# Expert layers of the latent tokens: streaming both whole tables and multiplying densely, with the first seven U parts multiplied while the gates are made

## The reference

```python
q = (xt @ lp["peer_wq"]).reshape(n_tok, PEER_HEADS, 2, PEER_HALF)
s = jnp.einsum("thmd,mhnd->thmn", q, lp["peer_keys"])
# per head: top 16 of 128 in each half, top 16 of their 256 sums
idx = ...   # key1 * 128 + key2, 8 heads x 16 picks per token
g = jax.nn.softmax(top_s, axis=-1)
act = jnp.einsum("td,thkd->thk", xb, u_tab[ib])
out = jnp.einsum("thk,thkd->td", jax.nn.gelu(act) * gb, v_tab[ib])
```

## Time and profile before

| | |
|---|---|
| median of three runs | 2433.51 us |
| the profiled execution's own time (its span, from the first to the last instruction) | 2689.8 us |
| TensorE matmul busy | 1510.1 us, 56% |
| VectorE busy | 1524.4 us, 57% |
| ScalarE busy | 281.3 us, 10% |
| POOL busy | 1466.1 us, 55% |
| moved by DMA | 969.43 MB, mean 360 GB/s |
| of it the gathers (queue 0) | 805.40 MB |
| mean granted TensorE clock | 0.721 |

### The profile page before, as it was taken

How to read it: one execution, slowest core, us unless ns; L and a number is a source line. 1 busy time by engine, 2 the same in 40 slices (tenths; PEclk the granted TensorE clock), 3 DMA queues, 4 the chain that set the end, 5 groups by cost and what they waited for, 6 DMA issues and landing times.

```text
span 2689.8 us, 20637 instructions
## 1 busy us (share of the span) xinstructions
PE 1510.1 (56%) x6676; PEld 682.0 (25%) x6676; DVE 1524.4 (57%) x4059; ACT 281.3 (10%) x715; POOL 1466.1 (55%) x1540
## 2 busy tenths in 40 slices
PE   6898668694244554554556866868400444442466
PEld 2464433371012110122312442354100100110012
DVE  0349974756886555455360965575776844446401
ACT  1321133010000110100000032211000000000000
POOL 0005445536665666666556635545676666667664
PEclk8889888896666665676768787878755655565568
DMA  9979998988999999999979988888899999999997
GB/s 360 411 320 379 395 388 324 365 306 318 357 397 411 412 388 379 371 410 411 389 286 374 364 341 314 324 313 296 318 399 373 343 383 375 358 374 383 378 357 271
DMA packets 238044, 969.43 MB, mean 360 GB/s; under 512 B 26314, under 2 KB 28746, under 8 KB 227954
## 3 DMA queue, kind: packets, MB, share of 16 engines
q0 software_dynamic: 221184, 805.40, 78.0%
q1 hardware_dynamic: 16754, 162.71, 14.9%
HBM read 964.87 MB, written 3.15 MB: 360 GB/s over the span
## 4 chain that ended last, share of the span: by engine, by line
DVE 27%; PE 24%; issue 15%; POOL 13%; another core or an unknown queue 11%; DMA 7%; ACT 2%; SPq 0%; DVEq 0%; ACTq 0%; POOLq 0%
PE acc L1077 8%; PE psum L1031 6%; DVE ring L1871 6%; POOL work L695 6%; POOL ring L695 5%; DVE work L1871 3%; PE psum L786 3%; DVE work L1463 2%; POOL wring L695 2%; DMA ring<-peer_v_in,vidx 2%; PE psum L796 2%; DVE work L1460 2%; DMA ring<-peer_u_in,idx 1%; DVE wring L1871 1%
## 5 line engine op out<-in xcount | busy, mean ns | idle before, releaser
L695 POOL DMA_INDIRECT ring<-peer_u_in,idx x415 | 396.5, 955 | 460.6 <-DVE idx L1566 208.0
L1871 DVE CUSTOM_DVE_ANT_0 ring<-ring,h_kept 128x1024 f32<-128x1024 f32 x415 | 488.9, 1218 | 126.3 <-DMA ring<-peer_u_in,idx 93.5
L695 POOL DMA_INDIRECT ring<-peer_v_in,vidx x392 | 378.5, 966 | 325.8 <-PE acc L1077 116.9
L1077 PE MATMUL acc<-ring,vw 128*32 128x512 f32 x1412 | 299.2, 778 | 276.6 <-DVE vw L1852 107.6
L1077 PE MATMUL acc<-work,vw 128*32 128x512 f32 x852 | 218.4, 794 | 325.5 <-DVE vw L1852 155.0
L1871 DVE CUSTOM_DVE_ANT_0 work<-work,h_kept 128x1024 f32<-128x1024 f32 x220 | 262.0, 1219 | 159.3 <-DMA work<-peer_u_in,idx 124.2
L695 POOL DMA_INDIRECT work<-peer_v_in,vidx x267 | 252.0, 944 | 144.8 <-issue 74.0
L695 POOL DMA_INDIRECT work<-peer_u_in,idx x220 | 207.1, 941 | 116.7 <-issue 58.9
L1031 PE MATMUL psum<-work,wring 128*128 128x256 f32 (+1 forms) x896 | 187.1, 369 | 49.5 <-issue 46.6
L786 PE MATMUL psum<-wring,work 128*128 128x512 f32 (+1 forms) x432 | 180.4, 575 | 32.4 <-issue 22.8
L1031 PEld LDWEIGHTS psum<-work,wring 128*128 128x128 f32 x896 | 160.3, 216 | 81.5 <-issue 62.0
(11 more groups left out here) (244 smaller groups left out, 2028.4 us busy)
## 6 DMA issues: line engine op xcount, KB each, us to landing
wring<-w_in_in SPq DMA_DIRECT2D x17, 2048.0 KB
wring<-peer_wq_in SPq DMA_DIRECT2D x14, 2048.0 KB
wring<-mod_w_in SPq DMA_DIRECT2D x10, 2048.0 KB
ring<-mod_w_in SPq DMA_DIRECT2D x9, 2048.0 KB, 12.2
wring<-w_out_in SPq DMA_DIRECT2D x8, 2048.0 KB
work<-mod_w_in SPq DMA_DIRECT2D x5, 2048.0 KB, 14.4
ring<-peer_u_in,idx POOLq DMA_INDIRECT x415
ring<-peer_v_in,vidx POOLq DMA_INDIRECT x392
```

Of the source, the lines that this page charges most:

```text
L695: nc.gpsimd.indirect_dma_start(slots[slot_of[n]], None, table, bass.IndirectOffsetOnAxis(ap=at[:, col + r:col + r + 1], axis=0))\
L1077: ins = mm(acc[half][lane:lane + QUAD, :], w[:, at:at + QUAD], two[j - pair][0][:, half * CHUNK:(half + 1) * CHUNK], start=(r == 0), stop= ...
L1871: V.tensor_tensor_reduce(held, held, h_kept[:, :], 1.0, 0.0, ALU.mult, ALU.add, dots[:, dots_at(k, t) + r:dots_at(k, t) + r + 1]).then_inc ...
```

## The change

Context steps keep the gathers. A latent step no longer gathers:

1. **Gates** (`dense_gates`, new pauses `("gates", t, i)`). For each tile the picks' key1, key2 and gates are transposed to one pick per partition. For each token, VectorE makes a 128 x 128 one-hot of key1 times the gate (scalar compare) and, for four tokens at once, a one-hot of key2; TensorE multiplies them to the 128 x 128 matrix of the token's gates over all experts; ScalarE copies four tokens' matrices from PSUM into a stage, and stores 32 tokens (2 MB) at a time in a DRAM tensor `dense_gates` (eight stores per step, 16.8 MB).
2. **Passes** (`experts`). The experts are streamed in 64 passes of two groups of 128. Event `p`: one 1 MB U part, 16 matmuls of 128 x 128 by 256 tokens, gelu by ScalarE. Event `w`: VectorE multiplies by the gates, from slices of 1 MB (four passes each) that POOL loads back. Event `m`: one 1 MB V part, 8 matmuls of 128 x 128 by 512 columns, into `acc` (tile 0) and `h_kept` (tile 1).
3. **Order.** The first seven `p` stand at the pauses of the gates. Then, for each pass c: `w` of c + 2, `m` of c, `p` of c + 7. 0.85 of step 1's events are spread over the dense part of step 2, the rest follows it; step 3's run after everything.
4. **Buffers.** U and V parts use five buffers of 1 MB in `ring`, in step 3 also four in `wring`. All are loaded by POOL with direct DMAs from tables laid out in parts.
5. Step 3's head start for tile 0 (`ahead`) is dropped; so are most lent slots and, for latent tiles, `idx` sums and `vidx`. The final norms of both latent tiles stand at the end, behind both sums.

```diff
+PAIR = 2
+PASSES = 128 // PAIR
+LEAD, READY, AHEAD = 7, 2, 7
+SLOTS = 5
+SLICE = 4
+GROUP = 32
...
-                self.ahead = k == 3
+                self.ahead = False
...
+        g_slices = [region(12336 + i * 2048, 2048) for i in range(2)]
+        acts = [hn[t][:, i * CHUNK:(i + 1) * CHUNK] for t in range(2) for i in range(2)]
+        acts += [region(16432 + i * CHUNK, CHUNK) for i in range(3)]
+        parts = [ring[:, i * PAIR * D:(i + 1) * PAIR * D] for i in range(SLOTS)]
+        parts += [held[:, i * PAIR * D:(i + 1) * PAIR * D] for held in wring for i in range(2)]
+        def part_slots(k):
+            return len(parts) if k == STEPS - 1 else SLOTS
...
+            def load_part(kind, k, c):
+                to, landed, _ = part(kind, k, c)
+                slot, n = part_at(kind, k, c), part_no[kind, k, c]
+                if n - part_first[k] >= part_slots(k):
+                    pool.wait_ge(*part_left(slot, k, n))
...
+                nc.gpsimd.dma_start(to, io["u_parts" if kind == "p" else "v_parts"][k // 2, c]).then_inc(landed, 16)
+            def load_slice(k, n):
+                if n < 2:
+                    pool.wait_ge(*after("g_stored0", k, 6))
+                    pool.wait_ge(*after("g_stored1", k, 7))
+                else:
+                    pool.wait_ge(*after("wt", k, (n - 1) * SLICE - 1))
...
+            def dense_gates(st):
+                for t in range(st.T):
+                    yield ("gates", t, 0)
...
+                    for q in range(P // 4):
+                        p = job(pe, "G", k, t, q)
+                        pe.wait_ge(*after("hot", k, t, q))
+                        hot = st.L.onehot[q % 2]
+                        for u in range(4):
+                            ins = mm(p[:, u * P:(u + 1) * P], hot[:, u * P:(u + 1) * P], hot[:, 512 + u * P:512 + (u + 1) * P],
+                                     start=True, stop=True)
+                        ins.then_inc(*made("G", k, t, q))
+                        if q % 8 == 7:
+                            yield ("gates", t, 1 + q // 8)
+            def experts(kind, k, c):
+                if kind == "p":
...
+                    pe.wait_ge(landed, count)
+                    for j in range(PAIR):
+                        for b in range(DB):
+                            ins = mm(p[:, j * 256:(j + 1) * 256], w[:, b, j * P:(j + 1) * P], st.L.hT[1][:, b, 0:256],
+                                     start=(b == 0), stop=(b == DB - 1))
...
+                    pe.wait_ge(landed, count)
+                    pe.wait_ge(*after("wt", k, c))
+                    w = acts[c % len(acts)]
+                    for j in range(PAIR):
+                        for t in range(2):
+                            for half in range(2):
+                                ins = mm(sum_of(t, half), w[:, j * 256 + t * P:j * 256 + (t + 1) * P],
+                                         rows_of[:, j, half * CHUNK:(half + 1) * CHUNK],
+                                         start=(c == 0 and j == 0), stop=(c == PASSES - 1 and j == PAIR - 1))
...
+                        carry(stage.rearrange("p (n t) -> p t n", t=GROUP)[:, q % 8 * 4:q % 8 * 4 + 4, :],
+                              bank("G", k, t, q)[:, :].rearrange("p (t n) -> p t n", t=4), "G", k, t, q)
+                        if q % 8 == 7:
+                            act.wait_ge(*taken("G", k, t, q))
+                            act.dma_start(io["dense_gates"][st.layer, g], stage).then_inc(*mark(stored, k, g, n=16))
...
+                        for u in range(4):
+                            n = 4 * q + u
+                            d(V.tensor_scalar(hot[:, u * P:(u + 1) * P], c("count"), picks[:, n:n + 1],
+                                              picks[:, 2 * P + n:2 * P + n + 1], ALU.is_equal, ALU.mult))
+                        wide = [P, 4, P]
+                        V.tensor_tensor(hot[:, 512:1024].rearrange("p (u n) -> p u n", u=4), c("count").unsqueeze(1).broadcast_to(wide),
+                                        picks[:, P + 4 * q:P + 4 * q + 4].unsqueeze(2).broadcast_to(wide), ALU.is_equal)\
+                            .then_inc(*mark("hot", k, t, q))
...
+                    V.tensor_tensor(w, w, g[:, first:first + PAIR, :, :], ALU.mult).then_inc(*mark("wt", k, c))
...
+def expert_events(st):
+    events = []
+    for c in range(-READY, PASSES):
+        for kind, at in (("w", c + READY), ("m", c), ("p", c + LEAD)):
+            if 0 <= at < PASSES and (kind, at < AHEAD) != ("p", True):
+                events.append((kind, st.k, 0, at))
+    return events + [("x", st.k, 0, 0)]
+BESIDE_SHARE = 0.85
...
-            left = events_two(steps[k])
-            plan["exp", 1] = plan["exp", 1] + left[:EARLY]
-            left = left[EARLY:]
+            for c, (t, i) in enumerate([(0, 1), (0, 2), (0, 3), (0, 4), (1, 1), (1, 2), (1, 3)]):
+                plan["gates", t, i] = [("p", steps[k].k, 0, c)]
+            left = expert_events(steps[k])
         elif k and k < len(steps):
...
+            most = int(len(left) * BESIDE_SHARE)
+            spread(plan, names, left[:most])
             plan[None] = left[most:]
```

More of the change, by code:

```diff
@@ L272, in latent_layout @@
             L.half_f = [region(18072, 128), region(16664, 128)]
+            L.stage = [region(i * 4096, 128 * GROUP) for i in range(2)]
+            L.onehot = [region(8192 + i * 1024, 1024) for i in range(2)]
+            L.pickT = [region(12824 + t * 384, 384) for t in range(2)]
             return L
@@ L344, in mod_column @@
             return columns_of[:, at:at + 1]
-        def dots_at(k, t):
-            return (sum(st.T for st in steps[:k]) + t) % 2 * PICKS
-        vw_places = [held[:, :] for held in vw] + [region(16384 + i * CHUNK, CHUNK) for i in range(2)]
         def vw_of(k, t, q):
-            return vw_places[q % (4 if k == STEPS - 1 else 2)]
+            return vw[q % 2][:, :]
         def job(pe, *key):
@@ L661, in _, with row_used, gather_row @@
         def _(pool):
-            for n, (kind, k, t, r) in enumerate(stream):
+            def row_used(key):
+                pool.wait_ge(u_used if key[0] == "u" else v_used, used_after[key])
+            def gather_row(kind, k, t, r):
+                n = row_no[kind, k, t, r]
                 col = (steps[k].X + t) * PICKS
@@ L1169, in opening @@
                 yield "start"
+                if st.first and k:
+                    act.wait_ge(*after("g_stored0", k - 1, 6))
+                    act.wait_ge(*after("g_stored1", k - 1, 7))
                 if st.first:
@@ L1551, in choose @@
                     dve.wait_ge(*after("newv", st.layer))
+                if st.lat and t == 0:
+                    dve.wait_ge(*full("ps", k, st.T - 1, 3))
                 for m in range(2):
@@ L1557, in choose @@
                 settle()
+                at = (st.X + t) * PICKS
+                if st.lat:
+                    half_f = [kept.bitcast(F32)[:, at:at + PICKS] for kept in (idx, vidx)]
                 for m in range(2):
@@ L1631, in dense @@
                         .then_inc(*mark("par_lam", st.layer))
+                if st.first and k:
+                    dve.wait_ge(*after("g_stored0", k - 1, 6))
+                    dve.wait_ge(*after("g_stored1", k - 1, 7))
                 d(V.memset(st.L.xraw[:, :, 0:2], 0.0))
@@ L1956, in pauses_of @@
         names += [(("exp", t), 2)]
+    if st.lat:
+        names += [(("gates", t, i), 2) for t in range(T) for i in range(5)]
     return names
@@ L2037, in gather_plans @@
         plan = {}
-        def part(first, last):
-            return names[labels.index(first):labels.index(last) + 1]
         if k and k < len(steps) and steps[k].T == 2:
```

294 lines of the change are left out of this document (197 added, 97 removed).

## The result

The kernel after takes **3208.32 us** (median of four runs, 3207.61 to 3209.81) against 2433.51: a ratio of 1.319, 95% interval 1.317 to 1.321. The forecast was 2300 us with a range to 2430, so both its size and its sign were wrong. The rival that comes nearest is "four passes" (3140 us), which had 1 chance in 100.

What follows compares the result with a forecast made beforehand. The prediction took moving gathered rows by DMA to bound the latent expert stages, and TensorE to bound them after the change. Four stages, 636 + 660 + 446 + 556 = 2298, gave a forecast of 2300 us, range 2190 to 2430.

Steps and rivals of the forecast that it cites:

- four passes: Rival: each matmul takes twice the time read, 840 us more, or the clock stays at 1.2 GHz; 3140 us, chance 0.01.
- TensorE's price per matmul: Loops of expert passes: 0.216 us per 256-column and 0.433 us per 512-column matmul, 6.92 us per pass, 419 us per loop.
- matmuls of 256 and 512 columns 0.216 and 0.433 us apart: Sign for being right: spacing of TensorE's matmuls in the passes, as priced from the profile before.
- B above 700 us: Sign for being wrong: layer 0's latent expert work beside step 2, forecast 660 us against 768, exceeds 700.
- The trace disagrees: Dismissal of the documented four f32 passes on TensorE, by which a pass would be about 13.8 us, some 840 more overall.
- slower than before: Rival: the part stream in POOL's single queue starves TensorE, passes take some 9.4 us; 2600 us, chance 0.13.
- The gates: Making the gates before each loop: VectorE binds at 1.5 us per four-token group, 98 us plus 4 for turns per step.
- Seven U halves on TensorE, 24 us in all, fit: Early U parts beside the gates' making: per eight groups TensorE has 4.5 + 3.5 us against VectorE's 12.
- The hole: Wait between the last gate stores and the first passes of each loop: 14 us, bounds 8 to 30.
- D: Last stage, layer 1's latent expert work to the end: forecast 556 us (510 to 600) against 731 in the profile before.
- step 2 beside the passes: Step 2's own work added to layer 0's loop: 100 us of TensorE work plus 25 us waiting on its chains.
- Stages A and C: Steps 0 and 1; step 3's dense part beside step 2's context gathers: 636 and 446 us, scaled by 0.905 for timed runs.

## Why the prediction was wrong, point by point

**TensorE's price per matmul: this failed.** The step reads "32 of the first kind took 7.07 us and 64 of the second 27.73 us ... 0.216 and 0.433 us each, so 3.46 + 3.46 = 6.92 us per pass". The rows are right; their counts are instructions. L1007 with 64 is 32 matmuls of the code (two tiles, two halves, eight blocks). The cost is 0.433 and 0.867 us, a pass is 13.84, and 121 x 6.92 = 837 us are missing in the sum: with them it gives 3135. The other 73 us up to 3208 are the gates and the hole, less what other terms came out shorter.

The count could have been had from before. Its group of the very line that gave the price is this:

```profile
L1007 PE MATMUL psum<-wring,work 128*128 128x512 f32 x192 | 88.5, 622 | 3.2 <-ACT work L1294 3.2
```

The code issues 16 of these matmuls for each of the six tiles, 96 in all. Likewise before has 3072 instructions for the matmuls of L1077, of which the code issues two per gather, 1536 for 768 gathers. My description gave "4 matmuls" for each gather; it took the trace's number for the code's. The forecast then mixed units: it counted added matmuls in the code and priced them by the trace. The sign named for being right, "matmuls of 256 and 512 columns 0.216 and 0.433 us apart", had the same slip in it: the instructions of after do stand so far apart, and there are twice as many. Of the signs for being wrong, only "B above 700 us" came true (1136), and it could not tell the cause.

**"The trace disagrees" was the same mistake.** I found 1040 cycles per 512 columns and set this against the Trainium skill. The code's matmul is two such instructions: 0.867 us x 2.4 GHz = 2080 cycles for 512 columns. The Trainium skill ("FP8 and Floating Point Precision", TensorE Precision Notes) says that true FP32 takes four passes through the array. The trace agrees with it: 2080 is four times 512 and a little, and the bf16 U product took 1.91 us against 7.07. The chance of 0.01 was the worst number of the text. A factor of two against a stated rule should have led to a count, not to a verdict.

**The rivals' own working** priced this case at +840 us, rightly ("four passes", by its first reading; its second, a clock that stays at 1.2 GHz, did not happen, as the loops ran at 0.99 of 2.4). And "slower than before" had found the point of decision: at a pass of 8.0 us the gain is gone. The pass was 13.8, though not by starvation.

**The gates: the pace was right, the cover was not.** 1.63 us per group was forecast as 1.5. But "Seven U halves on TensorE, 24 us in all, fit" set TensorE's total against VectorE's and forgot the depth of the buffer between them. A block of 6.9 us (3.5 in my count) behind two buffers stalls the maker for 5.9. The totals were too low as well, by the same count: with a U part TensorE needs over 14 us between two stores (the window of the run with four buffers) against VectorE's 13.0, and not 8 against 12. The gates took 165 and 169 us, not 102, 130 us for both steps. ScalarE's copy took 1.06 us and not 0.60, still under 1.63.

**The hole** was 20 us, not 14. The timeline of POOL in D shows its parts:

```profile
2339.80 0.91 POOL L746 DMA_DIRECT2D work<-dense_gates  x1 [166.25 <-DMA dense_gates<-work]
...
2341.58 0.56 POOL L736 DMA_DIRECT2D wring<-v_parts_in  x1
```

The last store was issued at 2333.0, POOL may fetch at 2339.8, VectorE has the first slice at 2346.6, and TensorE waits for the first V part, which stands behind the slices, until 2352.6. In B TensorE was busy for 12 of the 20 us with step 2's work, so most of the wait is D's. A load of V could have been issued before the slices; this was not tried.

**What held.** 768.7 MB for 768; a clock of 0.99; a loop bound by TensorE and not by DMA (its share 0.48 to 0.50 where 0.8 was forecast, as the pass is twice as long); no starvation by POOL (a part costs it 0.53 us, a slice 0.9); step 2 beside the passes 115 us for 125; the end 18 for 21.

**Stages A and C** came out at 624 and 403 for 636 and 446. They had been scaled by 0.905, the ratio of the timed runs to the profiled execution, since the latter's gathers looked stretched. Recording is not what stretches them, but gathers do differ between the two conditions, and by more than 0.905: in after A is 624 for 695 and C 403 for 497. One factor for both stages came within 12 and 43 us, which is in part luck.

**The range** left "four passes" out because one count was trusted. Had the count been reconciled, the same working would have given 3135 us and a forecast of slower.

## What to carry to other kernels

Before pricing added work by a row of the trace, reconcile the row's count with the code's: instructions per matmul, per copy, per gather. When a trace seems to contradict a documented rate by a whole factor, the unit is the first suspect. For work put on an engine beside a producer and consumer pair, compare the block's length with the buffers between them, and not only the engines' totals. Replacing gathers by a dense stream paid here only once the products were in bf16, where the stream of 5.6 us per pass and not TensorE's 13.8 was the bound.

## What the runs showed of the hardware

- An f32 matmul with 128-row operands appears as two TensorE instructions, of 0.216 us for 256 columns and 0.433 for 512 at a granted clock of 1.00; an f32 transpose as a single one (12 for 12 at L1129). A bf16 matmul is a single one too, a U product of 16 taking 1.9 us against 7.07 in f32.
- Stages that gather took 695 and 497 us on one chip and 624 and 403 in the first profile of the same kernel, while its loops of streamed passes, from the last store of gates to the sum, took 971 and 860 there and 972 and 859 in the first profile. A comparison of such kernels needs both on one chip: the ratio of after to before was 1.319 in one condition and 1.239 in the other.
- POOL issues a 1 MB direct load in 0.53 us where a gather of 0.52 MB costs it 0.95 to 0.99; in the loops of the bf16 kernel, whose loads round f32 to bf16, the DMA share was 1.04.
